# Sparse attention in sixteen units: the compressed branch rides along with the selected one, tiles 0 to 2 are scored as one piece over both heads

## The reference, cut to what matters

```
sc = einsum('bqghd,bngd->bghqn', qg, k_cmp) * scale
p_cmp = softmax(where(valid_c, sc, NEG)) * any(valid_c)
o_cmp = einsum('bghqn,bngd->bqghd', p_cmp, v_cmp)
ss = einsum('bqghd,bgqkld->bghqkl', qrg, k_sel) * scale      # causal
o_sel = einsum('bghqkl,bgqkld->bqghd', softmax(ss), v_sel)
sw = einsum('bqghd,bsgd->bghqs', qrg, k_w) * scale           # causal
o_win = einsum('bghqs,bsgd->bqghd', softmax(sw), v_w)
out = einsum('bsch,bschd->bshd', gates, stack([o_cmp, o_sel, o_win])) @ w_o
```

## Time and profile before

| | |
|---|---|
| median of 3 runs | 2735.23 us (2728.07 to 2737.54) |
| the profiled execution, its own time | 2727.23 us |
| its span from the first to the last instruction | 2725.1 us |
| TensorE busy in the span | 2491.4 us (91%) |
| stage of the sparse attention | about 855 us to 1102 us of the span |
| mean granted clock, whole span and 855 to 1106 us | 0.942 and 0.74 |

### The profile page before, as it was taken

The page is one execution under the profiler, slowest core; times in us unless marked ns, Lnnn a source line. Parts: engine busy times, 40 slices in busy tenths (PEclk is TensorE's granted clock), DMA queues, the critical chain, the costliest instruction groups (busy, mean ns, idle before and its releaser), DMA issues.

```text
span 2725.1 us, 36886 instructions
## 1 busy us (share of the span) xinstructions
PE 2491.4 (91%) x13831; PEld 1935.6 (71%) x13831; DVE 1331.4 (49%) x2001; ACT 908.6 (33%) x1691; POOL 1052.6 (39%) x992
## 2 busy tenths in 40 slices
PE   7999899999998989899999699988999999499996
PEld 5777688887576555688888588878988897344542
DVE  3343344433455555344334466662067641767674
ACT  3444322223112455322223333431145400345452
POOL 7553544443051001644444544434751275311122
PEclk8999999999997787999999899998999899599998
DMA  4111333333241000233331311111210130489997
GB/s 127 55 55 47 101 100 93 97 96 87 68 110 46 1 1 1 77 94 96 96 95 37 89 40 47 40 55 55 85 40 24 32 92 17 141 291 352 357 357 251
DMA packets 267868, 268.50 MB, mean 99 GB/s; under 512 B 13339, under 2 KB 198518, under 8 KB 267750
## 3 DMA queue, kind: packets, MB, share of 16 engines
q1 hardware_dynamic: 262998, 253.91, 29.3%
q0 software_dynamic: 4752, 12.98, 1.9%
HBM read 256.10 MB, written 10.75 MB: 98 GB/s over the span
## 4 chain that ended last, share of the span: by engine, by line
PE 80%; DVE 7%; ACT 4%; DMA 4%; issue 3%; POOL 2%; SPq 1%; POOLq 0%; DVEq 0%; ACTq 0%
PE psum L2552 16%; PE psum L2555 15%; PE psum L2556 15%; PE psum L2244 3%; PE psum L1465 3%; PE psum L2316 2%; PE psum L1303 2%; PE psum L1249 2%; PE psum L1288 2%; PE psum L2382 2%; PE psum L2202 2%; PE psum L881 2%; DMA ring_tile<-in_w_up 1%; PE psum L883 1%; PE psum L2208 1%
## 5 line engine op out<-in xcount | busy, mean ns | idle before, releaser
L2552 PE MATMUL psum<-x_hi,w_hi 128*128 128x264 f32 (+1 forms) x1536 | 526.6, 343 | 36.5 <-DVE x_lo L802 12.1
L2555 PE MATMUL psum<-x_lo,w_hi 128*128 128x264 f32 (+1 forms) x1536 | 516.4, 336 | 0.0
L2627 POOL TENSOR_TENSOR w_lo<-ring_tile,w_hi 128x1024 fp32r<-128x1024 f32 x128 | 307.8, 2405 | 381.1 <-ACT w_hi L2610 379.1
L840 POOL TENSOR_TENSOR w_hi<-ring_tile,one 128x256 fp32r<-128x256 f32 (+1 forms) x288 | 239.4, 857 | 520.6 <-PE psum L2556 463.3
L2552 PEld LDWEIGHTS psum<-x_hi,w_hi 128*128 128x128 f32 x1536 | 293.2, 191 | 74.8 <-issue 36.7
L2556 PE MATMUL psum<-x_hi,ring_tile_lo 128*128 128x264 f32 (+1 forms) x1088 | 340.9, 313 | 0.0
L2555 PEld LDWEIGHTS psum<-x_lo,w_hi 128*128 128x128 f32 x1536 | 293.5, 191 | 29.1 <-issue 1.2
L844 POOL TENSOR_TENSOR ring_tile_lo<-ring_tile,w_hi 128x256 fp32r<-128x256 f32 (+1 forms) x288 | 305.7, 1087 | 8.5
L2833 DVE TENSOR_TENSOR h<-psum,h 128x512 f32<-128x512 f32 x80 | 55.0, 692 | 337.3 <-PE psum L2556 270.1
L2610 ACT ACTIVATE w_hi<-ring_tile 128x1024 fp32r<-128x1024 f32 x128 | 135.0, 1057 | 251.7 <-PE psum L2556 240.9
L2556 PEld LDWEIGHTS psum<-x_hi,ring_tile_lo 128*128 128x128 f32 x1088 | 207.6, 191 | 11.8
(11 more groups left out here) (411 smaller groups left out, 5107.9 us busy)
## 6 DMA issues: line engine op xcount, KB each, us to landing
ring_tile<-in_mlp_w SPq DMA_DIRECT2D x128, 512.0 KB, 3.9
ring_tile<-in_w_gate SPq DMA_DIRECT2D x64, 512.0 KB, 7.3
ring_tile<-in_w_up SPq DMA_DIRECT2D x64, 512.0 KB, 7.2
ring_tile<-in_w_down SPq DMA_DIRECT2D x64, 512.0 KB, 7.7
ring_tile<-in_w_in SPq DMA_DIRECT2D x52, 512.0 KB, 3.9
ring_tile<-in_sb_w_qkv SPq DMA_DIRECT2D x24, 512.0 KB, 3.8
ring_tile<-in_nsa_w_kv SPq DMA_DIRECT2D x12, 512.0 KB, 3.6
ring_tile<-in_sb_w_o SPq DMA_DIRECT2D x8, 512.0 KB, 3.6
```

The source lines that it names most:

```text
L840: last = pool.tensor_tensor(hi[:, cols], raw[:, cols], one[:, :].broadcast_to([P, D // len(parts)]), ALU.mult)
L2552: upper = pe.matmul(dst, a_hi, b_hi, start=first, stop=False)
L2555: pe.matmul(dst, a_hi, b_lo, start=False, stop=False)
L2627: pool.tensor_tensor(lo, raw, hi.bitcast(F32), ALU.subtract).then_inc(split_w, 1)
```

## The change

The compressed branch has no unit of its own. There are 16 units, a selected one and a window one for each pair. The compressed scores of the next pair are made in the window unit as four products over all 128 partitions against `k_both`, which holds the keys of head 0 in the upper and of head 1 in the lower half, with zeros between; they land in one of the two banks of the transposes, which are now handed out as slots. Its softmax has tiles and semaphores of its own (`cmp_s`, `cmp_mm`, `cmp_blk`, `cmp_uu`, `cmp_ee`, `cmp_hh`), its transposes and its two value products are put into the selected unit, and its transposed probabilities have a tile of their own, `cmp_T`.

The scores come in two pieces, tile 3 and then tiles 1, 2 and 0. In the second, head 0 of tile 1 is paired with head 1 of tile 2, then head 0 of tile 2 with head 1 of tile 1, and all six masks come at the end. PE scores two units ahead in its list, and the weighing of a unit is cut in two, key blocks 0 and 2, then 1 and 3. ACT makes all exponentials of the next unit before it takes the first transposed group of this one.

```diff
-        PIECES = ((3,), (2, 0), (1,))
+        PIECES = ((3,), (1, 2, 0))
+        MAX_AT = {3: 1, 1: 2, 2: 4, 0: 4}
...
+            for n in range(3):
+                last = product(1, 0, n)
+                if n == 2:
+                    last.then_inc(ns_s, 1)
+                product(2, 1, n)
+            for n in range(3):
+                product(2, 0, n)
+                if n == 0:
+                    pe.wait_ge(ns_s, score_no(d, 0) + 1)
+                product(1, 1, n)
+            for n in range(3):
                 for hh in range(2):
-                    for n, (a, b) in enumerate(products):
-                        product(1, hh, a, b, n == 0)
-                    last = mask(1, hh)
-                    if hh == 0:
-                        last.then_inc(ns_s, 1)
-                        pe.wait_ge(ns_s, score_no(d, k))
+                    product(0, hh, n)
+            for i in (2, 1, 0):
+                for hh in range(2):
+                    last = mask(i, hh)
             last.then_inc(ns_s, 1)
+        def cmp_scores(pe, u):
+            dst = slot_bank(cmp_slot(u))
+            slot_taken(pe, cmp_slot(u))
+            for i in range(QT):
+                last = pe.matmul(dst[:, 2 * 32 * i:2 * 32 * i + 2 * N_CMP], q_raw[:, u, i * P:(i + 1) * P], k_both[:, u // 2, :],
+                                 start=True, stop=True)
+            last.then_inc(cmp_mm, 1)
...
+            for d in range(UNITS):
+                u, slc, more = d // 2, d % 2 == 0, d + 2 < UNITS
+                nsa_fill(pe, d, 0)
+                nsa_fill(pe, d, 1)
+                if more:
+                    nsa_scores(pe, d + 2, 0)
+                if not slc and more:
+                    cmp_scores(pe, u + 1)
+                nsa_fill(pe, d, 2)
+                if slc:
+                    nsa_fill(pe, d, 3)
+                if more:
+                    nsa_scores(pe, d + 2, 1)
+                if slc:
+                    cmp_fill(pe, u, 0)
+                else:
+                    nsa_fill(pe, d, 3)
+                nsa_fill(pe, d, 4)
+                pe.wait_ge(ns_t, fill_at(d, 3) + 1)
+                if slc and u:
+                    pe.wait_ge(ns_oe, u)
+                nsa_weigh(pe, d, (0, 2))
+                if slc:
+                    cmp_fill(pe, u, 1)
+                pe.wait_ge(ns_t, fill_at(d, 4) + 1)
+                last = nsa_weigh(pe, d, (1, 3))
+                if slc:
+                    cmp_weigh(pe, u)
...
         def nsa_dve(dve):
             dve.wait_ge(gate_x, 2)
+            for k in range(2):
+                nsa_maxima(dve, 0, k)
             for d in range(UNITS):
+                u, slc, more = d // 2, d % 2 == 0, d + 1 < UNITS
+                if not slc:
+                    cmp_normalise(dve, u)
+                    if u:
+                        nsa_out(dve, u - 1)
+                if more:
+                    nsa_maxima(dve, d + 1, 0)
+                if slc:
+                    cmp_softmax(dve, u)
                 nsa_normalise(dve, d)
+                if more:
+                    nsa_maxima(dve, d + 1, 1)
```

More of the change, by code:

```diff
@@ L1224, in both_banks, with product @@
             return (psum[:, 2:4, 384:512], bank[4][:, :].rearrange("p (h n) -> p h n", h=2), psum[:, 2:4, 0:384], psum[:, 0:2, :])[i]
[L1226 to L1227 removed]
         def nsa_scores(pe, d, k):
[L1230 to L1237, removed]
[L1238 to L1250 removed]
+            u, br = d // 2, 1 + d % 2
+            if d:
+                pe.wait_ge(ns_p, piece_no(d - 1, k))
+            products = ((qr_hi, k_hi), (qr_hi, k_lo), (qr_lo, k_hi))
+            def product(i, hh, n):
+                a, b = products[n]
+                return pe.matmul(score_bank(hh, i), a[HALF[hh], u, i * P:(i + 1) * P], b[HALF[hh], u // 2, br - 1, 0:P * (i + 1)],
+                                 start=(n == 0 and i != 0 and (i, hh) != (1, 1)), stop=False, skip_group_check=True)
             def mask(i, hh):
@@ new lines, in nsa_fill, with nsa_weigh @@
+        def nsa_fill(pe, d, k):
+            f = fill_at(d, k)
+            slot_taken(pe, fill_slot(f))
+            pe.wait_ge(ns_f, head_no(d, 0 if k < 2 else 1))
+            at = 0
+            for hh, j in FILLS[k]:
+                for i in range(j, QT):
+                    last = pe.transpose(slot_bank(fill_slot(f))[:, at:at + P], probs[d % 2][hh][:, PROB_AT[i] + j * P:PROB_AT[i] + (j + 1) * P], ident[:, :])
+                    at += P
+            last.then_inc(ns_tt, 1)
+        def nsa_weigh(pe, d, js):
+            u, br = d // 2, 1 + d % 2
+            for j in js:
@@ L1304, in nsa_weigh, with cmp_weigh @@
                                      probs_T[:, hh, PT_AT[j]:PT_AT[j] + CAUSAL_COLS[j]],
-                                     start=False, stop=(br == 2 and j == QT - 1), skip_group_check=True)
-            if br == 2:
-                last.then_inc(ns_o, 1)
+                                     start=(br == 1 and j == 0), stop=(br == 2 and j == QT - 1), skip_group_check=True)
+            return last
+        def cmp_weigh(pe, u):
+            pe.wait_ge(ns_t, cmp_fill_at(u, 1) + 1)
+            for hh in range(2):
+                pe.matmul(bank[7][HALF[hh], :], v_cmp[:, u // 2, :], cmp_T[0:N_CMP, hh, :], start=False, stop=False, skip_group_check=True)
```

234 lines of the change are left out of this document (118 added, 116 removed).

## The result

The change takes 2665.64 us (median of four runs, 2659.65 to 2669.28), the kernel before 2733.62 us (four runs on the same chip, 2728.07 to 2737.54). The ratio is 0.9751, with an interval from 0.9722 to 0.9779: 68 us faster, where 36.6 were forecast. The profiled execution of the change took 2669.28 us, the longest of the four.

A forecast was written before the change was run, and what follows sets the result against it. PE's work and its clock level were taken to set the rhythm. Seven periods, 7 x (30.0 - 26.1), plus 9.3 at the ends gave 36.6 us saved: 2690.6 from the 2727.2 execution, 2699 against the median 2735.2; range 2670 to 2720.

The forecast's parts named there:

- Score pieces: PE's scores of tiles 1, 2 and 0 in one piece: 2.4 us at full clock against 3.1 before.
- 1.4 us full per pair of heads: Full-clock PE time saved per pair of heads by the new scoring of tiles 1, 2 and 0.
- Compressed scores: Compressed branch on PE: half of the score products, 1.85 us to 0.93, saving a further 0.9.
- low share of 0.38: Part of each period with PE's clock low: two stretches of some 5 us, giving a period of 26.1 us.
- the prediction's own formula: Period of a head pair from low share x: P = 18.8 / (0.535 x + 0.83 (1 - x)).
- The walk: PE stepped against ScalarE at full clock: waits of 1.4 (selected unit), 1.8 (window unit), half a us before weighing; together 3.7.
- The 3.7 of before: PE's waits in a pair of the kernel before at full clock: 3.7 us of 24.8.
- the clock stays nearly full: Rival for PE's clock: x under 0.15, total 2674 to 2683 us, 2663 with shorter waits; chance 0.22.
- x = 0: No low-clock share of PE's period: P 22.6 us with the forecast waits, total 2674 us.
- the prediction's own signs: Wrong if mean clock is over 0.93 or under 0.74, PE waits pass 5 us per pair, or VectorE ends them.
- The rule on transposes: Trainium skill on PE: transposes don't count as activity for the clock; x would go towards 0.7, period to 30.1 us.
- The ends: Stage's start and tail: first transposes at 867.5 save 6.8 us, tail 15.5 against 18.0; together 9.3 us saved.

The follow-up runs named there:

- e2: The changed kernel with tiles 2, 0 and 1 scored as before, so the compressed branch's ride-along alone; 2684.06 us, ratio 0.9832 to the kernel before.
- e9: The changed kernel itself, unaltered, run again on another chip; 2659.32 us, ratio 0.9744 to the kernel before.
- e8: The kernel before with compressed scores as four products over 128 partitions against k_both in place of eight; 2715.15 us, ratio 0.9944.
- e6: The changed kernel with four small extra copies on ScalarE ahead of the takes in each unit; 2687.09 us, ratio 0.9834 to the kernel before.
- e3: The kernel before with each transpose of the selected and window units made twice into the same place; 2751.77 us, ratio 1.0092.
- e11: The changed kernel with compressed scores as eight half-array products and a PE wait between the heads; 2685.63 us, ratio 0.9824 to the kernel before.
- e5: The changed kernel with the compressed branch's transposes and value products in one block at the selected unit's end; 2675.09 us, ratio 0.9795 to the kernel before.
- e1: The kernel before with only the new score pieces (tile 3, then tiles 1, 2 and 0); 2712.84 us, ratio 0.9948.
- e10: The changed kernel with takes 0 and 1 ahead of all six exponentials of tiles 1, 2 and 0; 2666.07 us, ratio 0.9758 to the kernel before.

## Why the prediction fell short

**The direction and the place** were right: PE and its clock set the rhythm, takes behind exponentials are what PE waits for, and VectorE, ScalarE and GpSimd hide. What ends PE's waits is ScalarE in every group shown above.

**Score pieces.** The second piece was put at 2.4 us and measured 1.86. The six masks at the end cost 0.35. The prediction had four at 0.11 each, from the pair at 950.00 behind which the products of the next tile start 0.22 us later. But that distance isn't the price of two masks: where transposes follow, a pair takes 0.12 or 0.13, as these rows of before show (to 950.83 in the earlier trace rows for the second):

```profile
948.18 0.29 PE L1253 MATMUL psum<-future_neg_bf,ident_bf 128*128 128x128 bf16 x2
948.30 0.39 PE L1288 MATMUL psum<-ident,probs_a 128*128 128x128 f32 x2
...
950.70 0.28 PE L1253 MATMUL psum<-future_neg_bf,ident_bf 128*128 128x128 bf16 x2
```

So masks cost 0.06 us each in both kernels, and what the change saves is the way from a pair of masks to the next products. The eighteen products took 1.51 us, some 0.2 less than their part of the sum, and the wait of 0.15 for the first head of tile 1 did not show. So the term "1.4 us full per pair of heads" measured 2.4 (e2 against e9) to 2.5 (2 x (3.1 - 1.86)).

**Compressed scores.** 0.93 us forecast; the four products start at 884.27 and the next transposes 0.94 us later. The term was right as a time. That the products it replaced also weighed on the clock (e8) was not in it.

**Clock, the step that failed.** I held that both waits are long enough for the clock to fall, twice a pair, some 5 us each time, and chose a low share of 0.38 between the ends 0 and 1. It is 0 in the middle of the stage, in two executions of the kernel (the change and e9). In the prediction's own formula that step makes P 26.1 and not 22.6, 7 x 3.5 = 24.5 us in seven periods. Two things in it were wrong. The waits were walked too long, and longer ones do bring a fall back: with a wait of 1.81 us ahead of the compressed scores e6 has one in each pair. And even such waits don't make a low share of 0.38: with 1.8 and 1.6 us e6 has one fall of 3.4 us a pair, a share of 0.14, and a period of 24.13.

**Waits of PE, mis-sized.** Forecast were 1.4 and 1.8 us and half a us before the weighing, 3.7 together; measured on the mean 0.86, 1.01 and 0.26, 2.1 together, 1.6 us less in a period. The walk gave PE 2.9 us of work against ScalarE's 4.8 in the window unit; in the trace it is some 3.5 against 4.6. Of ScalarE's part the chain shows where the difference lies: the exponentials run from 879.72 to 883.74, 4.0 us and not 4.2, and a take holds PE up for 0.48 + 0.04 and not 0.6. PE's part is longer in part because ScalarE's last take ends some 0.3 us before the compressed value products begin, and not with them. The 3.7 of before, with which the sum was compared, rests on the 52% of the whole stretch; with the 48% of the seven periods the same formula gives 4.4.

So the case "the clock stays nearly full", at a chance of 0.22, happened; its sum was 2663 for P = 21, and P is 21.12. PE is busy 95.11 / 5 = 19.0 us of it, and 19.0 + 2.1 = 21.1. The prediction's work was 18.8, although the score pieces are cheaper, so other groups are dearer. The low end of the range, 2670, took in x = 0 with the waits as walked (2674); what it left out was x = 0 together with shorter waits. By the prediction's own signs it was wrong too: the mean clock of the stage, 0.95, lies over 0.93.

**Other forecasts.** The rule on transposes played no part: the clock rises behind them (e3).

**The ends.** The start was right: first transposes at 868.49, forecast 867.5. The tail was put at 15.5 us and is 19.5. I had counted PE's work down, but at the end VectorE is the one waited for. Its normalising of `probs_b` takes 2.95 us in place of 1.27, from when GpSimd splits the output weights, and the maxima stand behind it, and behind these ScalarE's exponentials and its take, for which PE waits 4.04 us. The clock, full until then, falls at 1021.5 and stays at 0.50 for 6.8 us, where one low us was forecast. Windows view of the change:

```profile
1019.00:1025.00 6.00, 1.96 (x10) 1.72 (x10) 5.76 (x13) 4.52 (x15) 5.92 (x10) 0.74 0.00 0
```

The trace of before has the same slow rows in its last pair, so this was there to be read; how much of the 4 us is GpSimd's wasn't tried.

**Sum.** Forecast 7 x (30.0 - 26.1) + 9.3 = 36.6. Measured 60.7 + 5.8 - 1.5 = 65.0 in the stage. The seven periods gave 60.7 where 27.3 were forecast, 33.4 us more, of which some 24 are the clock's and the rest the shorter waits'. The ends gave 4.3 and not 9.3, so an error of 5 us there hid part of it.

**What stays open.** The ride-along keeps the clock up (e2), and each of half-array products (e11), a block (e5) and longer waits (e6) costs one short fall. None of them alone brings back the low time of before, some 14 us a period. Which of them together does wasn't tried. In the other direction, the score pieces alone (e1) and the full-array compressed scores alone (e8) each bring the 17.1 us of most pairs down to 6.8. What a fall needs, beyond these examples, the runs don't show: in e5 and e10 pairs with the same work and the same waits differ in whether it comes. That the change's own waits are short enough is seen in two traces, and not shown for every execution. The turn of its own that the compressed unit had on VectorE and ScalarE wasn't tried either; that it matters is only argued.

## What to carry to other kernels

When a stage runs partly at the lower clock, find where it falls and what PE does in the few microseconds around: waits of 1.0 us passed here, one of 1.8 did not, and those of 1.3 to 1.6 went either way; and products over half of the array next to such a wait came with a fall that cost more than their time. If a forecast hangs on a wait of that size, price both outcomes and let the range hold both. Once the clock is up, look at what PE waits for and move single instructions on the engine that releases it: two takes, moved ahead of four exponentials, were worth 1.5 us of 21.1, and ahead of six, nothing.

## What was not expected of the hardware

- Four normalising instructions of VectorE (128x512, f32) take 1.27 us in the middle of the stage and 2.95 beside GpSimd's split of weights. Timeline of the change, VectorE and GpSimd, and then of the kernel before, VectorE:

```profile
951.68 1.27 DVE L1464 TENSOR_SCALAR probs_b<-probs_b,factor 128x512 f32<-128x512 f32 x4
...
1014.56 2.56 POOL L841 TENSOR_TENSOR ns_w_hi<-ring_tile,one 128x256 fp32r<-128x256 f32 x4 [184.29 <-PE psum L1268]
```

```profile
1051.84 1.27 DVE L1392 TENSOR_SCALAR probs_b<-probs_b,factor 128x512 f32<-128x512 f32 x4
...
1083.28 2.90 DVE L1392 TENSOR_SCALAR probs_b<-probs_b,factor 128x512 f32<-128x512 f32 x4
```

  The Trainium skill, "SBUF — State Buffer", SBUF: two separate sides, says that GpSimd and VectorE, the latter in a 2-port mode or with two SBUF inputs against a GpSimd read, take turns on a shared pair of ports, each holding it for a whole instruction. By that rule VectorE's rows would grow just where GpSimd's lie beside them; the trace agrees so far, 1.27 to 2.95, a growth of 1.68 us beside GpSimd's 2.56 for four. Whether VectorE ran in such a mode the trace doesn't show, and no run took GpSimd's work away.
- A mask (bf16, 128 columns) goes at 0.06 us, in a row of six (0.35 us) as in the pairs of before ahead of transposes (0.12 and 0.13); ahead of the next tile's products such a pair took 0.22.
- PE's clock rose from 0.50 to 1.00 behind 3.6 us of nothing but transposes (e3), and stayed at 1.00 behind microseconds with PE 25% busy (the change).
- In e11 it fell to 0.50 while PE was 100% busy in the records, from 912.2 on. Before that lay a wait of 1.01 us, 2.2 us of products over half of the partitions, and 1.3 us of transposes and scores. That PE is busy at the moment doesn't hold the clock; which of the stretches before counted, the run doesn't tell.
